# Prompt attention: TensorE takes the older group's transposes and value products first in each step, and the new score product last

## The reference, cut to what matters

```python
s = q @ kc.T * scale + tbl[..., bucket(dist)];  p_cmp = softmax(where(dist >= 0, s, NEG))   # 63 compressed blocks
s = q @ ks.T * scale + bias;                    p_slc = softmax(where(dist >= 0, ...))      # selected blocks
s = q @ kw.T * scale + bias;                    p_win = softmax(where(0 <= dist < 512, ...))# sliding window
o = gate_cmp * (p_cmp @ vc) + gate_slc * (p_slc @ vs) + gate_win * (p_win @ vw)
```

## Time and profile before

| | |
|---|---|
| median of 3 runs | 1777.36 us (1770.89 to 1778.14) |
| the profiled execution: own time, span | 1780.58 us, 1778.6 us |
| granted TensorE clock, mean | 0.95 |
| TensorE busy | 1605.4 us (90%) |
| VectorE busy | 737.6 us (41%) |
| ScalarE busy | 454.5 us (26%) |
| GpSimd busy | 199.6 us (11%) |
| prompt attention | 490.7 to 832.0 us |

### The profile page before, as it was taken

The page is one execution under the profiler, slowest core; times in us unless marked ns, Lnnn a source line. Parts: engine busy times, 40 slices in busy tenths (PEclk is TensorE's granted clock), DMA queues, the critical chain, the costliest instruction groups (busy, mean ns, idle before and its releaser), DMA issues.

```text
span 1778.6 us, 21737 instructions
## 1 busy us (share of the span) xinstructions
PE 1605.4 (90%) x8327; PEld 1318.4 (74%) x8327; DVE 737.6 (41%) x1379; ACT 454.5 (26%) x948; POOL 199.6 (11%) x216
## 2 busy tenths in 40 slices
PE   6997599889877888998997999999999999999995
PEld 4654355443554565665996999999999999999994
DVE  3159403000198777664125223424334234143257
ACT  2100011310355555555114211111111111111112
POOL 1008612200132211100002000000000000000001
PEclk9999799989989898988997999999999999999997
DMA  6812001243100000003210102112022021120112
GB/s 167 232 41 48 1 2 36 72 131 94 60 1 1 1 1 1 1 1 125 68 38 11 48 21 66 34 44 63 21 57 66 13 63 46 34 66 21 54 36 116
DMA packets 133972, 89.01 MB, mean 50 GB/s; under 512 B 32194, under 2 KB 128025, under 8 KB 133793
## 3 DMA queue, kind: packets, MB, share of 16 engines
q1 hardware_dynamic: 131377, 78.73, 15.3%
q0 software_dynamic: 2496, 8.88, 1.8%
HBM read 78.85 MB, written 13.19 MB: 52 GB/s over the span
## 4 chain that ended last, share of the span: by engine, by line
PE 72%; DVE 9%; DMA 4%; issue 4%; POOL 4%; ACT 3%; SPq 3%; DVEq 0%; ACTq 0%; POOLq 0%
PE psA L944 15%; PE psB L944 15%; PE psC L944 15%; PE psD L917 5%; PE psA L795 4%; PE psC L631 4%; POOL newcols L1740 3%; PE psA L752 3%; PE psB L752 2%; DMA bias_scratch<-dT 2%; DVE wide L1575 2%; SPq L530 2%; DMA wraw<-in_w_gu 1%; PE psD L631 1%; DVE nmax L1491 1%
## 5 line engine op out<-in xcount | busy, mean ns | idle before, releaser
L1592 DVE TENSOR_TENSOR wL<-wraw,wH 128x1024 fp32r<-128x1024 f32 (+1 forms) x140 | 100.3, 717 | 227.7 <-ACT wH L1232 227.6
L917 PE MATMUL psD<-probTb,kvtok 128*128 128x512 f32 x264 | 140.8, 616 | 16.8 <-ACT probTb L1087 16.7
L944 PE MATMUL psA<-fH,wH 128*128 128x352 f32 x416 | 139.2, 335 | 6.0 <-DVE fL L1626 3.4
L1232 ACT CAST wH<-wraw 128x1024 fp32r<-128x1024 f32 (+1 forms) x140 | 90.2, 648 | 197.8 <-PE psC L944 86.9
L944 PE MATMUL psA<-fL,wH 128*128 128x352 f32 x416 | 135.7, 326 | 0.0
L944 PE MATMUL psA<-fH,wL 128*128 128x352 f32 x416 | 135.6, 326 | 0.0
L944 PE MATMUL psB<-fH,wH 128*128 128x352 f32 x416 | 134.5, 323 | 1.2 <-DVE fL L1642 1.2
L1723 POOL TENSOR_TENSOR small<-small 128x1 f32<-128x1 f32 (+1 forms) x27 | 18.6, 694 | 1033.3 <-DVE small L1374 1033.2
L944 PE MATMUL psC<-fH,wH 128*128 128x352 f32 x416 | 134.2, 322 | 0.0
L944 PE MATMUL psB<-fH,wL 128*128 128x352 f32 x416 | 133.5, 321 | 0.0
L944 PE MATMUL psC<-fL,wH 128*128 128x352 f32 x416 | 133.4, 321 | 0.0
(11 more groups left out here) (316 smaller groups left out, 3411.0 us busy)
## 6 DMA issues: line engine op xcount, KB each, us to landing
wraw<-in_w_gu SPq DMA_DIRECT2D x44, 512.0 KB
wraw<-in_w_down SPq DMA_DIRECT2D x88, 128.0 KB
pages<-in_cache_cmp_kv SPq DMA_DIRECT2D x32, 128.0 KB, 2.4
xt<-in_x_prompt SPq DMA_DIRECT2D x8, 512.0 KB, 6.6
out_y_prompt<-featT SPq DMA_DIRECT2D x8, 512.0 KB, 2.6
out_new_win_sample<-in_cache_win_kv POOLq DMA_DIRECT2D x1, 4064.0 KB, 28.6
kvw<-in_w_in SPq DMA_DIRECT2D x1, 3168.0 KB, 33.2
kvw<-in_x_prompt SPq DMA_DIRECT2D x6, 512.0 KB, 9.1
```

The lines of the kernel that those rows point to most:

```text
L917: mm = pe.matmul(bank[6 + g], kvtok[:, kt, vc:vc + P], pt, start=(br == 1 and g == 0 and x == 0), stop=(br == 2 and g == 1 and x == len(g_ ...
L944: mm = pe.matmul(bank[3 * par + n][:, 0:cw], wt[:, par, k, :], mv[:, k, at:at + cw], start=(k == 0 and mv is mH and wt is wH), stop=(k == ...
L1232: sc_.copy(wH[:, par, 0:nk, :], wraw[:, par, 0:nk, :]).then_inc(s["wH_done"], 1)
L1592: dve.tensor_tensor(wL[:, par, 0:nk, :], wraw[:, par, 0:nk, :], wH[:, par, 0:nk, :].bitcast(F32), ALU.subtract).then_inc(s["wL_done"], 1)
```

## The change

In each step TensorE issues the score product of the new group behind the transposes and value products of the older group, not ahead of them. The order of the other engines' instructions is the same as before.

```diff
             for m, r, scored, tiles in steps():
-                if scored:
-                    p_score(m, r)
                 for n, x in tiles:
                     if n in DENSE:
                         if x == 0:
                             pe.wait_ge(s["scaled"], GQ * (DENSE[n] + 1))
                         turn(("t", n, x), [(P * r, P, prob(n, r)[:, P * x:P * x + P]) for r in range(GQ)])
                     else:
                         pe.wait_ge(s["cmp_scaled"], GROUPS[n][0] + 1)
                         turn(("t", n, x), [(P * r, P, pcmp[:, r].rearrange("p g n -> p (g n)")) for r in range(GQ)])
                     if pend:
                         p_values(*pend.pop())
                     pend.append((n, x))
+                if scored:
+                    p_score(m, r)
             p_values(*pend.pop())
```

## The result

| | before | changed |
|---|---|---|
| median of 4 runs | 1774.9 us (1770.89 to 1778.14) | 1839.37 us (1837.48 to 1842.68) |
| profiled execution: own time, span | 1780.58, 1778.6 us | 1842.68, 1840.9 us |
| mean granted clock | 0.950 | 0.954 |

The ratio is 1.0366, 95% interval 1.0336 to 1.0396: the change makes the kernel 3.7% slower. Forecast were 1837 us and 3.4% more.

What follows compares the result with a forecast made beforehand. In prompt attention's heavy steps the chain ran on TensorE alone, from one value product to the next. Profiled 1780.6 + 55.5 us of waits + 4 for the clock = 1840.1; the median is 3.2 lower: 1837 us, range 1822 to 1855 (0.74).

Steps and rivals of the forecast that it cites:

- V: TensorE's value product of a transposed tile, taken as 0.86 us; it waits for ScalarE's copy of that tile.
- T: TensorE's transposing of a tile (four 128x128), taken as 0.43 us.
- D: Block 7's fourth group, two tiles in each step: waits of 2.05 us, scores 5.6 us apart instead of 3.5.
- B1 to B2: Second and third steps of block 7's second group, two tiles each: wait 1.5 us each, 4.7 apart instead of 3.2.
- B0: First step of a block's second group: transposes and cmp value product fill the score's wait, giving back about 0.7 us.
- A: A block's first group; in block 7 its scores have no tiles between them and wait for exp as before.
- C0: First step of the third group: value product waits 3.5 us more in blocks 7 and 6, 2.2 in block 5.
- C2: Third step of the third group: value product waits 1.6 us for the copy behind the cmp score's exp, blocks 5-7.
- the second rival: The clock falls to its lower level in the new waits: 1865 us, up to 1885; chance 0.10.
- Part of the loss is covered: Rival: one-tile steps, the small blocks and C2 hide their latency; 25 to 35 us remain, 1802 to 1812; chance 0.10.
- Nothing changes: Rival: value product and score only swap places, TensorE's lead was never used; 1777 us; chance 0.03.
- faster: Rival: transposes and value products fill the time a score waits for exp, gaining 8 us, 1769; chance 0.03.

Runs made afterwards that it cites:

- 3: Changed kernel with ScalarE copying the step's tiles before exp of the step before, instead of after: 1775.35 us, ratio 1.0004 to the kernel before.
- 4: Changed kernel with value products two tiles behind the transposes instead of one, ScalarE's order untouched: 1788.46 us, ratio 1.0082 to the kernel before.
- 5: Changed kernel, but in steps with two tiles the score stands between the tiles: 1797.84 us, ratio 1.0117 to the kernel before.
- one-tile steps alone: Kernel before with the new order only in steps with one tile: 1797.87 us, ratio 1.0118.
- experiment 1: Kernel before with the new order only in steps with two tiles: 1815.61 us, ratio 1.0227.

## Why the prediction was right

**The mechanism** was as put: a V waits for a copy that stands behind exp(k-1), and the change took a score, a T and a V, or more, out of the work ahead of it. Three experiments show it from different sides: the copies moved off exp (3), the V moved off the copy (4), the score moved half a step (5). Each leaves the new order, in whole or in part, and takes away the waits at D, in 3 by an edit on ScalarE alone.

**The sizes of the steady steps** held. D in block 7: forecast 2.05 us of wait and a pitch of 5.6, measured 5.55 (3.52 before, so 2.03; the record of the wait says 1.76, because without a wait V starts 0.43 us behind its T, before T's record of 0.60 has ended, and because V's own record is 0.11 longer behind a wait). B1 to B2 of block 7 came 4.69 us apart, forecast 4.7. Exp starts 0.04 us behind its maximum, as forecast. The sum over the waits of value products was forecast as some 70 us in over 50 places, measured 69.2 in 56.

**Block by block** the forecast was 1, 2, 3, 4, 5.2, 9.0, 13.1 and 18.2 us, measured 0.2, 0.6, 2.2, 8.0, 6.5, 12.1, 17.0 and 19.9. Blocks 0 to 3 together lost 11.0 us, forecast under 15. The stage lost 66.5 us where 59.5 were forecast with the clock, and the rest of the kernel was 4 us shorter, which is no effect of the change that anything here shows. So luck has a part in 1837 against 1839 us. Three terms were mis-sized.

The first is B0, which I had at -0.7 us, since T, the cmp V and T would fill a wait. In the changed kernel, block 7:

```profile
803.84 0.50 PE L897 MATMUL psA<-kH,qS 128*128 128x512 f32 x1 [0.62 <-ACT wide L1217]
...
807.03 0.60 PE L631 MATMUL psC<-cpk,wide 128*128 128x128 f32 x4
...
808.85 1.11 ACT L1217 ACTIVATE wide<-psA,nmax 128x1024 f32<-128x1024 f32 x1 [2.65 <-DVE nmax L1491]
...
809.95 0.58 ACT L1087 COPY probTb<-psC 128x512 f32<-128x512 f32 x1
...
810.58 2.07 PE L917 MATMUL psD<-probTb,kvtok 128*128 128x512 f32 x2 [2.95 <-ACT probTb L1087]
...
830.48 2.05 PE L917 MATMUL psD<-probTb,kvtok 128*128 128x512 f32 x2 [2.89 <-ACT probTb L1087]
...
832.32 1.84 PE L887 MATMUL psB<-kcBD,qT 128*128 128x128 f32 x8
...
837.15 1.13 PE L917 MATMUL psD<-probTb,kvtok 128*128 128x512 f32 x2 [1.25 <-ACT probTb L1087]
```

The last score of A (its first matmul is the first line) was followed at once by T, the cmp V and T at full clock, so this work was over at 807.6; exp of A3, held up by the weighting of A2, ended at 810 (808.85 + 1.11 and its read), the copy stood behind it, and V waited 2.95 us. In block 6 it was 2.57. The prediction saw T, the cmp V and T fill a wait of the score and did not hold them against the exp of A3, which the weighting delays. In the kernel before this work ran at the lower clock (766.5 us ends the slow stretch of the earlier trace rows); at that clock it would have lasted some 5 us instead of 2.7, by an estimate, and covered most of the wait. These waits are most of block 6's excess of 3.9 us. In block 7, whose excess is 1.7 us, other terms were too high: C0 waited 0.65 and 2.89 us, 3.5 together, where 3.8 were forecast, and C2 1.25 instead of 1.6.

The second is the clock. It cost about what I put, but elsewhere: in the stretches at a granted clock of 0.50 TensorE was busy 63.9 us in the changed kernel and 54.4 in the kernel before, and half of the difference, 4.7 us by an estimate, is what the lower clock added. At 830.48 above, behind the wait of 2.89 us, a V took 2.05 us and the cmp score 1.84, where they take 1.02 and 1.05 at full clock: about 1 us a piece at the lower level (1.2 GHz). From block 3 on, such rows stand behind seven of the eight waits of V of over 2.5 us, behind one of them only in part. The D steps with a wait of 1.76 us in each turn of 5.55 us stayed at full clock throughout, so the second rival, a clock that falls in every serial step, is refuted: the mean granted clock in the stage was 0.92, and 0.91 before. The reason that the prediction gave for its 4 us held only in part: of the waits that the earlier trace rows counts, the ones of 2.45 and 3.5 us passed at full clock, but another one had a slow V behind it in the kernel before already:

```profile
582.62 2.07 PE L917 MATMUL psD<-probTb,kvtok 128*128 128x512 f32 x2 [2.57 <-ACT probTb L1087]
```

The Trainium skill, page "TensorE: Matmul & The Clock Gate", section "HAM oscillation — how this bites in real kernels", describes a loop that throttles in each turn; TensorE waited some 3 to 5 us for a transfer in each turn there. The prediction left this length out when it said that by that rule the D steps would be slow: their waits of 1.76 us are shorter, and they neither bear the page out nor contradict it. The long single waits here did bring a slow stretch behind them, the short regular ones did not.

The third is block 3, forecast 4 us, measured 8.0. I took the small blocks by going down from block 4. The windows show the granted clock at 0.85 there (0.96 before), and TensorE's busy time rose from 30.9 to 36.9 us, 6.0 of the 8.0, behind two waits of 2.94 and 3.53 us: its excess is mostly clock and not count. Blocks 0 to 2 lost less than forecast. There VectorE is the fuller engine, as argued, but the granted clock was also higher in them than before (0.95 against 0.90 in block 2), and the runs do not part the two.

**The rivals.** "Part of the loss is covered" did not come: one-tile steps alone lost 21 us. "Nothing changes" and "faster" fell with the time and with the D steps. The gain that the last rival hoped for, T and V filling the scores' waits, is absent: those waits are 23.6 us instead of 23.9.

**What I had not seen** is how far the weighting and the lead multiply: 16 us of the kernel before are due to where the four weightings stand, 37 of the changed one. I had listed the weighting for C0 alone, with 3.5 + 3.5 + 2.2 = 9.2 us over three blocks and 1.3 in block 4, and in D2 with 0.5 a block. That the total came out right rests partly on terms whose errors cancel.

## What to carry to other kernels

When a stage is a ring of engines (score, maximum, exp, copy, value product), moving an instruction within one engine's step changes how far that engine is ahead of the others: count the work between the producer and the first instruction behind it that needs the result, before and after, and hold it against the latency read from one turn, which gave the pitch of a step here to 0.05 us. Let no copy that frees another engine stand in a queue behind work that waits for a third one (that edit on ScalarE's queue was worth 64 us once TensorE's lead was gone; it was not tried on the kernel before), and look for bursts between two links of the chain (moving four multiplications of VectorE behind the next maximum gained 0.9% for the kernel before).

## What the runs showed of the hardware

That TensorE kept its full clock through 22 us of D steps with a wait of 1.76 us in each 5.55 us, but ran at the lower level right behind most single waits of 2.5 us and more (10 us at 0.66 around the wait of 2.94 us in block 3), was not expected in this form. Why two of them, of 2.57 us in block 6 and 2.56 in block 4, came out differently (a V of 1.12 and one of 2.08 us) the runs do not settle. Nor is it the place in the kernel that decides: the wait of 2.89 us at C0 of block 7 had the lower level behind it in the changed kernel (0.58 from 830.4 to 834.5 us), and the same wait of 2.89 us in experiment 1 the full clock (1.00 from 808 to 812 us).
